# Output weights of cross-attention summed in place by GpSimd, chunk by chunk, and their seven products reordered

## The reference, cut to what matters

```python
def memory_cross_attention(h, mem_n, wq, wkv, wo):
    q = (h @ wq).reshape(B, S, X_HEADS, X_DH)
    k, v = jnp.split(mem_n @ wkv, 2, axis=-1)
    s = jnp.einsum('bshd,bmhd->bhsm', q, k) * (X_DH ** -0.5)
    p = jax.nn.softmax(s, axis=-1)
    o = jnp.einsum('bhsm,bmhd->bshd', p, v).reshape(B, S, D)
    return o @ wo                       # 256 x 1024 by 1024 x 1024

x = x + memory_cross_attention(...)     # then x feeds the router and the experts
```

## Time and profile before

| | |
|---|---|
| median of 3 runs | 990.96 us |
| span of the profiled execution | 991.6 us |
| PE busy | 970.2 us, 98% of the span |
| DVE busy | 511.3 us, 52% |
| ACT busy | 148.9 us, 15% |
| GpSimd busy | 134.5 us, 14% |
| the seven products in layer 0 / layer 1 | 252.4 to 282.3 us / 731.9 to 761.9 us |

### The profile page before, as it was taken

The page is one execution under the profiler, slowest core; times in us unless marked ns, Lnnn a source line. Parts: engine busy times, 40 slices in busy tenths (PEclk is TensorE's granted clock), DMA queues, the critical chain, the costliest instruction groups (busy, mean ns, idle before and its releaser), DMA issues.

```text
span 991.6 us, 12328 instructions
## 1 busy us (share of the span) xinstructions
PE 970.2 (98%) x4989; PEld 526.7 (53%) x4996; DVE 511.3 (52%) x890; ACT 148.9 (15%) x348; POOL 134.5 (14%) x131
## 2 busy tenths in 40 slices
PE   8999999999999999999999999999999999999996
PEld 7668445669575453333334954465974433333332
DVE  2523486766553435443554567686656533334333
ACT  3202000411011111111112100042020111011112
POOL 3066132000010000000001943210000100000000
PEclk9999999999999999999999999999999999999999
DMA  9963301963379999999999260077397899999994
GB/s 357 425 242 131 131 1 37 391 254 125 130 291 383 417 424 418 421 423 420 421 419 422 109 254 1 2 312 281 128 358 278 339 421 419 421 421 420 421 413 164
DMA packets 45119, 293.65 MB, mean 296 GB/s; under 512 B 5504, under 2 KB 5760, under 8 KB 13312
## 3 DMA queue, kind: packets, MB, share of 16 engines
q1 hardware_dynamic: 38288, 266.36, 66.1%
q10 hardware_dynamic: 5616, 22.24, 5.7%
q0 software_dynamic: 1152, 4.19, 1.1%
HBM read 283.33 MB, written 9.44 MB: 295 GB/s over the span
## 4 chain that ended last, share of the span: by engine, by line
PE 94%; DMA 2%; DVE 1%; POOL 1%; issue 1%; ACT 0%; POOLq 0%; DVEq 0%; SPq 0%; ACTq 0%
PE bank L1073 21%; PE bank L1153 11%; PE bank L616 9%; PE bank L634 6%; PE bank L846 6%; PE bank L636 6%; PE bank L708 5%; PE bank L900 5%; PE bank L964 5%; PE bank L736 5%; PE bank L1112 3%; PE bank L606 2%; PE bank L1107 2%; PE bank L772 2%; PE bank L918 1%; PE bank L934 1%
## 5 line engine op out<-in xcount | busy, mean ns | idle before, releaser
L1073 PE MATMUL bank<-ring,hT 128*64 128x512 f32 x704 | 181.3, 593 | 0.0
L1073 PEld LDWEIGHTS bank<-ring,hT 128*64 128x64 f32 x704 | 58.2, 137 | 92.3 <-issue 92.3
L616 PE MATMUL bank<-ring,hT 128*128 128x512 f32 x192 | 85.6, 599 | 0.0
L2091 DVE TENSOR_TENSOR x<-bank,x 128x512 f32<-128x512 f32 x64 | 43.3, 692 | 46.0 <-PE bank L1112 46.0
L1479 POOL TENSOR_TENSOR sm<-sm 128x1 f32<-128x1 f32 x4 | 1.0, 239 | 449.5 <-ACT both L1271 241.5
L616 PEld LDWEIGHTS bank<-ring,hT 128*128 128x128 f32 x192 | 35.5, 190 | 40.7 <-issue 40.2
L1153 PE MATMUL bank<-ring,xs 128*64 128x512 f32 x224 | 56.7, 595 | 0.0
L846 PE MATMUL bank<-ring,hT 128*128 128x512 f32 x128 | 56.3, 595 | 0.1
L1153 PE MATMUL bank<-ring,og 128*64 128x512 f32 x128 | 42.5, 595 | 0.0
L1073 PE MATMUL bank<-work,hT 128*64 128x512 f32 x96 | 42.2, 593 | 0.0
L1509 POOL TENSOR_TENSOR ring<-ring 128x2048 f32<-128x2048 f32 x8 | 36.8, 4599 | 29.1 <-DMA ring<-in_w_mix 19.4
(11 more groups left out here) (325 smaller groups left out, 1660.8 us busy)
## 6 DMA issues: line engine op xcount, KB each, us to landing
ring<-in_w_experts SPq DMA_DIRECT2D x140, 1024.0 KB, 17.1
ring<-in_w_mix SPq DMA_DIRECT2D x60, 1024.0 KB, 15.8
work<-in_w_experts SPq DMA_DIRECT2D x20, 1024.0 KB, 15.0
late<-in_w_mix ACTq DMA_DIRECT2D x4, 2048.0 KB, 9.8
late<-in_w_experts SPq DMA_DIRECT2D x8, 1024.0 KB, 14.9
keys<-in_w_experts SPq DMA_DIRECT2D x8, 1024.0 KB, 16.8
both<-in_w_experts SPq DMA_DIRECT2D x8, 1024.0 KB, 21.4
ring<-in_w_experts SPq DMA_DIRECT2D x10, 512.0 KB, 16.3
```

What stands on the lines that cost most here:

```text
L616: last = nc.tensor.matmul(b[:, :], lhs[:, c, m * P:(m + 1) * P], w[:, c, :], start=(c == 0), stop=(c == C - 1))
L1073: last = nc.tensor.matmul(banks[2 + g][b2 * CAP:(b2 + 1) * CAP, :], rows_T_of(p)[:, c, b2 * CAP:(b2 + 1) * CAP], w, start=(c == 0), stop=( ...
L2091: V.tensor_tensor(xv, banks[OUT_BANK[n][m]][:, :], xv, ALU.add).then_inc(r_added[L], 1)
```

## The change

The block sums and the order of the products are altered, and the two token halves trade places in them. DVE's four weight sums are gone, with the slot `P_SUMS`. GpSimd makes four sums instead, each of them over one of its own inputs (`in_place`), in four chunks of 128 x 512; a chunk that PE still reads raw is waited for (`p_chunk`, or `job_done` for the last), and PE waits for each chunk of a sum that it reads. `rows_turned(0)` and the first squares wait for a new semaphore, `half_done`, which the first of the three additions of p_6 raises.

```diff
-SAME_SLOT = {P_SUMS: Q_SUMS}
-SUMS_AFTER = {"hq": H_SUMS, "av": SUMS, "q1": Q_SUMS, "p1": P_SUMS}
+SUMS_AFTER = {"hq": H_SUMS, "av": SUMS, "q1": Q_SUMS}
...
-            "o0": "wo01", "o1": "wo11", "q0": "q_3", "q1": "q_4", Q_SUMS: "q_5", "p0": "p_2", "p1": "p_3", P_SUMS: "p_4"}
+            "o0": "wo01", "o1": "wo11", "q0": "q_3", "q1": "q_4", Q_SUMS: "q_4", "p0": "p_7", "p1": "p_4"}
...
                 wait_job(eng, l, LAST_USE[old])
+                if old == "p0":
+                    eng.wait_ge(p_weight_sum, 16 * (l + 1))
...
-                        "p_1": (rows_block(1, 0), 0, weight_block(L, "p0", 0), 0), "p_2": (rows_block(1, 1), 0, weight_block(L, "p0", 1), 0),
-                        "p_5": (token_sums(0), 2, weight_block(L, P_SUMS, 0), 1), "p_6": (token_sums(1), 3, weight_block(L, P_SUMS, 1), 2),
-                        "p_7": (token_sums(2), 1, weight_block(L, "p1", 0), 3), "p_3": (token_sums(3), 4, weight_block(L, "p1", 1), 0),
-                        "p_4": (rows_block(0, 1), 0, weight_block(L, "p0", 0), 4)}[name]
+                        "p_1": (rows_block(0, 0), 0, weight_block(L, "p1", 0), None), "p_2": (rows_block(0, 1), 0, weight_block(L, "p1", 1), None),
+                        "p_5": (token_sums(0), 1, weight_block(L, "p1", 0), 0), "p_6": (token_sums(1), 2, weight_block(L, "p0", 1), 2),
+                        "p_7": (token_sums(2), 4, weight_block(L, "p0", 0), 1), "p_3": (token_sums(3), 3, weight_block(L, "p0", 1), None),
+                        "p_4": (rows_block(1, 1), 0, weight_block(L, "p1", 1), 3)}[name]
...
                     for c in chunks:
+                        if summed is not None:
+                            pe.wait_ge(p_weight_sum, 16 * L + 4 * summed + c + 1)
                         last = nc.tensor.matmul(...)
+                        if summed is None and c < 3:
+                            last.then_inc(p_chunk, 1)
...
-                p_seventh("p_1")
+                p_seventh("p_1", range(2))
                 memory_values(1)
-                for i in (7, 6, 5, 4):
+                p_seventh("p_1", range(2, 4))
+                for i in (5, 2, 3, 6):
                     p_seventh(f"p_{i}")
-                p_seventh("p_2", range(2))
-                rows_turned(0, "p_4")
-                p_seventh("p_2", range(2, 4))
+                p_seventh("p_7", range(2))
+                rows_turned(0)
+                p_seventh("p_7", range(2, 4))
                 logits(0)
-                p_seventh("p_3", range(3))
+                p_seventh("p_4", range(3))
...
+                def in_place(i, dst, one, two, reader=None):
+                    if i >= 2:
+                        pool.wait_ge(p_weight_sum, 16 * L + 4 * i)
+                    for c in range(4):
+                        if reader and c < 3:
+                            pool.wait_ge(p_chunk, 9 * L + 3 * RAW.index(reader) + c + 1)
+                        elif reader:
+                            wait_job(pool, L, reader)
+                        minus(dst[:, c, :], one[:, c, :], two[:, c, :], ALU.subtract).then_inc(p_weight_sum, 1)
+
+                in_place(0, p11, p12, p11, "p_1")
+                in_place(1, p12, p22, p12)
+                in_place(2, p22, p22, p11, "p_3")
+                in_place(3, p21, p21, p22, "p_2")
                 norm(2)
...
-                p_weights(1, pt1, p12, p11)
-                p_weights(2, pt2, p22, pt1)
                 q_sum("q_7", 1, 0, "q_5")
-                p_weights(3, p12, p22, p12)
...
+                p_tokens(1, token_sums(0), rows_block(1, 0), rows_block(1, 1), ALU.add)
+                p_tokens(2, token_sums(1), token_sums(0), rows_block(0, 0), ALU.subtract)
+                p_tokens(3, token_sums(3), rows_block(0, 1), token_sums(1), ALU.subtract)
+                p_tokens(4, token_sums(2), rows_block(0, 0), rows_block(1, 0), ALU.subtract)
+                p_sum("p_1", (0, 1))
+                p_sum("p_5", (1, 0))
...
+                p_sum("p_2", (0, 1))
+                p_sum("p_3", (0, 0))
...
+                V.tensor_tensor(x[:, 0, 0:W], bank("p_6")[:, :], x[:, 0, 0:W], ALU.add).then_inc(half_done, 1)
+                p_sum("p_6", (1, 1), (1, 0))
...
                 rows_T("t5", 0, 24)
-                p_sum("p_2", (1, 0))
+                p_sum("p_7", (1, 0), (1, 1))
                 choose(0)
```

More of the change, by code:

```diff
@@ L74, in job_list @@
     jobs += [(f"pt0{jb}", "D") for jb in range(2)] + [("sx11", "A"), ("px0", "D"), ("px1", "A")]
-    jobs += [(f"pt1{jb}", "D") for jb in range(2)] + [("p_1", "D"), ("px2", "D"), ("px3", "A")]
-    jobs += [(f"p_{i}", "D") for i in (7, 6, 5, 4)]
-    jobs += [("t5_00", "D"), ("t5_01", "D"), ("p_2", "D"), ("rt0", "D"), ("rank0", "D"), ("p_3", "D"), ("t5_10", "D"), ("t5_11", "D"), ("rt1", "D")]
+    jobs += [(f"pt1{jb}", "D") for jb in range(2)] + [("px2", "D"), ("px3", "A")]
+    jobs += [(f"p_{i}", "D") for i in (1, 5, 2, 3, 6)]
+    jobs += [("t5_00", "D"), ("t5_01", "D"), ("p_7", "D"), ("rt0", "D"), ("rank0", "D"), ("p_4", "D"), ("t5_10", "D"), ("t5_11", "D"), ("rt1", "D")]
     return jobs + [("rank", "D")]
@@ L88 @@
 FIRST_ROWS = (0, 1)
-OPENED_AT = {"wo00": "et0", "wo10": "et0", "wo01": "et2", "wo11": "et2", "p_2": "t5_00"}
-ONTO = {"h_6": "h_1", "h_7": "h_6", "h_4": "h_7", "h_3": "h_5", "q_6": "q_1", "q_7": "q_6", "q_4": "q_7", "q_3": "q_5", "p_6": "p_1", "p_4": "p_7", "p_3": "p_5"}
+OPENED_AT = {"wo00": "et0", "wo10": "et0", "wo01": "et2", "wo11": "et2", "p_1": "px2", "p_7": "t5_00"}
+ONTO = {"h_6": "h_1", "h_7": "h_6", "h_4": "h_7", "h_3": "h_5", "q_6": "q_1", "q_7": "q_6", "q_4": "q_7", "q_3": "q_5", "p_6": "p_1", "p_3": "p_5"}
 def bank_plan(more):
@@ L1001, in layers_from @@
                 close(nc.tensor.matmul(b[:, 0:NE], before[:, :], chosen[:, 0, :], start=True, stop=True))
-                p_seventh("p_3", range(3, 4))
+                p_seventh("p_4", range(3, 4))
                 def gather(m, c2):
@@ L1570, in _ @@
                 norm(1)
+                p11, p21, p12, p22 = (weight_block(L, name, k) for name in ("p1", "p0") for k in range(2))
+                for name in ("p0", "p1"):
+                    for half in range(2):
+                        wait_loaded(pool, L, name, half)
+                RAW = ("p_1", "p_2", "p_3")
+                def in_place(i, dst, one, two, reader=None):
[11 more added lines that the diff above has]
+                in_place(3, p21, p21, p22, "p_2")
                 norm(2)
@@ L1990, in p_sum @@
                     emptied(last)
-                p_sum("p_1", (1, 0))
                 values_kept(2)
@@ L2032, in _ @@
                 emptied(V.tensor_tensor(rank[:, 0, :], base16, bank("rank0")[:, 0:N_EXPERTS], ALU.add))
-                p_sum("p_3", (1, 1))
+                wait_emptied(dve, L, "p_7")
+                p_sum("p_4", (1, 1))
                 def slots(m):
@@ L2046, in _ @@
                 slots(0)
-                wait_emptied(dve, L, "p_3")
+                wait_emptied(dve, L, "p_4")
                 rows_T("t5", 1, 24)
```

64 lines of the change are left out of this document (26 added, 38 removed).

## The result

The changed kernel takes 993.84 us (median of 20 runs, 992.40 to 996.63), the kernel before 991.24 us (20 runs, 990.67 to 994.90). The ratio is 1.0019, with a 95% interval of 1.0010 to 1.0028: the change costs about 1.9 us (the two medians alone lie 2.6 apart), which is clear of the noise and still less than the 0.5% that the prediction called a visible difference. The time forecast was 992.9.

The account below looks back on a forecast made before the run. PE was taken to bound the kernel, without gaps. Waits of 0.9 us in p_6 and 0.1 for the choice made 1.0 us a layer, 2.0 in all: forecast 992.9 us, range 990.3 to 996.6.

Parts of the forecast that it names:

- No gain to be had: Products and expert stages: PE runs without a gap, so removed DVE sums and the earlier load are worth 0.
- DVE's four sums: Weight sums removed from DVE, 9.1 us a layer: not in the chain, so worth 0.
- the early load: Load after the freed slot: 2 MB, 5.0 us of transfer, lies 21 us earlier once a layer; worth 0.
- The rival in which transfers set the pace: Expert stages run at the transfers' pace: earlier load gives up to 2 x 5.0 us, 981 at best; chance 0.04.
- The wait in p_6: PE waits in p_6 for GpSimd's third sum: 0.9 us a layer, between 0.2 and 2.8.
- The disturbance: DVE's second to fourth token sums beside GpSimd's chunks: GpSimd loses 3 or 4 x 0.23 = 0.8 us.
- "So no wait" in p_5: GpSimd's first sum, read by p_5: fourth chunk done at 261.4, PE wants it at 262.07; wait 0.
- the upper rival: Port locked both ways: each DVE token sum holds GpSimd 0.69 us, p_6 waits 2.8; 5.8 us in all; chance 0.12.
- The first token sum: DVE's first token sum, for p_5: starts at 258.52, ends at 259.21, needed at 259.50; cover 0.3 us, cost 0.
- One addition more: DVE, ahead of the router's choice: two additions take 1.29 us, PE loses about 0.1 us a layer, between 0 and 0.3.
- Fourth sum, `norm(2)`, `half_done`: After p_6: GpSimd's fourth sum covered by 4 us, `norm(2)` by 1.5; `half_done` 1 us early; no PE wait.
- From span to time: Profiled span goes from 991.6 to 993.6 us; taken as 0.6 above the runs' median, so the runs give 993.0.

Follow-up runs that it names:

- experiment 7: Kernel before, without its four weight sums; the four products that read them read raw weight blocks: 992.68 us, ratio 1.0003 to before.
- 5: Changed kernel, but the slot of Q_SUMS is given to the next expert load only when p_6 is done: 993.83 us, ratio 1.0023 to before.
- experiment 6: Changed kernel plus three more DVE token sums into an unread buffer behind p_5's addition, in layer 0 alone: 995.29 us, ratio 1.0028 to before.
- experiment 4: Changed kernel, GpSimd's second sum as one 128 x 2048 operation, DVE's fourth token sum behind p_5's addition: 993.30 us, ratio 1.0015 to before.
- Experiment 3: Changed kernel with the second addition of p_7 moved behind the router's choice of half 0 on DVE: 993.29 us, ratio 1.0017 to before.
- Experiment 1: Kernel before, profiled once more without an edit: 991.48 us, ratio 1.0004 to before.
- experiment 8: The repaired kernel: changed kernel, sums by DVE in place, second behind p_5's addition, choice ahead of p_7's second addition: 991.72 us, ratio 0.9990 to before.

## Why the prediction was right, and where it erred

**No gain to be had: right, shown.** Three of its zeros were tested: DVE's four sums (experiment 7: intervals equal within 0.01 us), the early load (5: within 0.02 us up to p_1 of layer 1), and the transfers' pace in the experts (PE busy for the same 19.96 and 20.00 us). The rival in which transfers set the pace falls with 5.

**The wait in p_6: right in place, 0.52 us and not 0.9.** The start of the third sum came out right (267.8) only because two wrong terms cancelled. GpSimd's chunks come every 1.23 to 1.25 us when undisturbed, not 1.38: the 0.08 us between operations of the earlier trace rows don't stand between these chunks, and 1.296 was the mean of four chunks of 1.26 to 1.27 and four of 1.33. The shortest row (1.26) would have been the better choice. Over the six chunks from p_1's third to the end of the second sum that is 7.4 us, where 8.3 were laid out. The disturbance was mis-sized the other way: 0.41 to 0.44 us for each of four token sums (experiment 6, and GpSimd's four chunks beside them, 258.71 to 265.31 in the timeline, less 4 x 1.23 us, over four), 1.7 us where 0.8 were taken. Together: 258.71 + 7.4 + 1.7 = 267.8, measured 267.81, forecast 267.7. The third sum, undisturbed, then needed 4.9 us and not 5.4. It ends at 272.82, 0.2 us after the 272.6 at which PE, already 0.25 late, could use it. The rest of the 0.52 was a term that the forecast lacks. PE's loads for a chunk run beside the matmuls ahead of it; one that must wait for the sum can't, and its 0.30 us (271.65, 272.87) stand open on PE's path. That is arithmetic from the rows, 0.2 + 0.3 = 0.5, and p_5 below agrees with it; no run took the load away.

**"So no wait" in p_5: wrong, 0.25 us.** This wait was forecast as nothing, and two terms were missing. The forecast had the first sum's fourth chunk end at 261.4. The disturbance was counted for the second sum, not for the first, whose last two chunks stand beside the first three token sums. They took 1.57 and 1.68 us and ended at 261.96. By the forecast's own measure that would still have been in time, since it wanted this chunk at 262.07. But the weight load has to come first: it was due at 261.50 and came at 262.05, and its 0.30 us were no longer hidden. The forecast measured lateness against the start of the matmul, and not against the load ahead of it.

**The port.** DVE's sum took 1.64 us, about a chunk of GpSimd's beside it (1.65), and 3.65 us beside a whole-block sum (experiment 4): DVE waits until GpSimd is between two operations, as the forecast had it. The Trainium skill (SBUF — State Buffer, "SBUF: two separate sides") says that the pair of ports is an exclusive lock in which "the other fully blocks". For DVE's side the trace agrees. For GpSimd's the price is 0.41 us a sum in experiment 6, and not DVE's whole 0.69. By the rule the upper rival (5.8 us) would have come true; it did not, but the trace stands nearer to it (0.41) than to the 0.23 that the forecast took. The 0.23 was misread, too. It spreads the 0.70 us by which 14.38 exceeds 13.68 over three DVE sums, but the third of them lasts until 557.94, past the end of GpSimd's last operation (543.02 + 14.38 = 557.40):

```profile
553.05 4.89 DVE L1718 TENSOR_TENSOR xs<-hT 128x512 f32<-128x512 f32 x1
```

Taken one by one in the timeline, GpSimd's three operations last 4.52, 4.86 and 4.84 us. Only the last two begin while a DVE sum ends, and each is about 0.33 us longer. Over two sums the same row gives 0.35 us each, near the 0.41.

**The first token sum: right within 0.03 us.** It starts at 258.50 (forecast 258.52), and PE uses it at 259.32, as planned. Its weight load waits for the sum until 259.25, and this may be the 0.03 us by which the stretch to p_2 exceeds 5.15 even in the repaired kernel (5.18). GpSimd's chunk began 0.2 us behind it, so the race was not lost.

**One addition more: right in kind, 0.21 and not 0.1 us.** Experiment 3 takes exactly this away. DVE took up the logits at 279.62 in the timeline after the change and at 279.42 in experiment 3, and the delay passed whole to PE. The forecast counted on 0.2 us of cover that wasn't there, between the choice's end (280.97 + 0.17) and PE's matmul at 281.35 in the chain. The timeline of before has it at 281.20, 0.06 behind the choice, and its weight load already waited for the choice:

```profile
281.19 0.10 PEld L1001 LDWEIGHTS bank<-chosen,before 128*128 128x128 bf16 x1 [0.67 <-DVE chosen L2024]
281.20 0.18 PE L1001 MATMUL bank<-chosen,before 128*128 128x16 bf16 x1
```

So there was no cover at all, and every delay of the choice reached PE; the forecast took the start from the coarser view.

**Fourth sum, `norm(2)`, `half_done`: right.** PE doesn't wait between 275.71 and 278.3 in the chain.

**From span to time: wrong, and harmless by luck.** The forecast set the profiled span 0.6 us above the median of the runs and took both as the same kind of number. Experiment 1 shows that the time is the span plus 1.85 us, and that the first profile was a sample more than 2 us slow. The two errors cancel, since the forecast only added its 2.0 us to the median in the end; measured are 1.9 by the ratio and 2.1 by the layers. Against its own number, 992.9, the median of 993.84 is 0.9 high; 0.3 of that is the kernel before, 991.24 over 20 runs and 990.96 over the first three.

The terms, forecast and measured, in us a layer:

| | forecast | measured |
|---|---|---|
| wait in p_5 | 0 | 0.25 |
| wait in p_6 | 0.9 | 0.52 |
| later choice | 0.1 | 0.21 |
| choice to half 1 | 0 | 0.07 |
| early load, DVE's sums removed | 0 | 0 |
| both layers | 2.0 | 2.1 |

The mechanism held: PE waits for GpSimd's chunks, and a little for the choice. That the total came within 0.1 us is in part luck: 0.38 too much in p_6 stands against 0.25, 0.11 and 0.07 too little elsewhere.

## What to carry to other kernels

When work moves from an idle helper engine to another, price it against the one engine that never waits: taking 9.1 us a layer off DVE was worth nothing, while a sum that was 0.2 us late in front of PE cost 0.5, since the weight load behind it is no longer hidden. Chunk by chunk hand-over needs a producer that is faster than its reader or a reader that comes later: GpSimd at 1.25 us a chunk can't feed PE at 0.86 when the reader follows directly behind the product that frees the input (experiment 4 got back a third of the stall, DVE in experiment 8 all but 0.04 us of it). And compare intervals inside a stage, not spans: here two spans of one kernel differed by 2.3 us and hid a change of 2.

## What the runs showed of the hardware

- DVE's sums of 128 x 512 with both inputs in SBUF and GpSimd's chunks of that size all but take turns: 1.65 us for a pair of them, where 0.69 and 1.25 are needed alone. Each costs DVE about 1 us and GpSimd 0.41 us, so side by side they are only 0.3 us quicker than one after the other.
- DVE's wait grows with the length of GpSimd's operation: beside one of 128 x 2048 its sum took 3.65 us (experiment 4) and 4.89. GpSimd's loss stays small: an operation that begins while a DVE sum ends took 4.84 to 4.86 us in the stretch of the earlier trace rows instead of 4.52, and 4.78 in experiment 4.
- Between the transposes of half 1 in layer 1 and the first matmul behind the gathered rows (L1153 before, L1163 after) the ten profiles take 26.3 to 30.4 us, though no edit here adds or takes work there (the kernel of experiment 7 may gather other rows, since its values differ). Two things go with it. The three that take 26.3 to 26.4 (after, before once more, second sum whole) show a clock of 1.00 in 768:772 and no transfer in the chain; the four whose chain waits for the gathered rows, as in the earlier trace rows, take 28.2 to 30.4; the other three have only the lower clock (in 768:772, two of them also ahead of it) and take 27.2 to 28.4. In experiment 3's profile the clock was at its higher level in 768:772, but the wait for the gathered rows was long: PE stood idle for 2.26 us ahead of their transposes, and these then took 1.97 us for eight, which take 0.87 in the chain after the change. The chain:

```profile
785.11 6.70 DMA xs<-by_slot
791.81 0.04 issue
791.86 1.97 PE bank L1108 x8
```

And the same kernel's stretch behind the wait, with a granted clock of 0.50, the level of 1.2 GHz:

```profile
792.00:794.00 2.00, 2.00 (x10) 1.85 (x10) 0.83 (x2) 0.00 (x0) 0.00 (x0) 0.50 1.05 438
```

These two go with the scatter of single profiles. No experiment took either away, so that they cause it, and what sets the landing, stays open.
